# Decay exponents of the mixing loop read from rows of running sums instead of summed by TensorE; another order of the first weight splits

## The reference, cut to what matters

```python
def ssd_scan(xs, dt, da, bm, cm, s0, strict):
    def step(s, inp):
        xc, ac, bc, cc = inp
        acum = jnp.cumsum(ac, axis=1)
        seg = acum[:, :, None] - acum[:, None, :]
        lmat = jnp.exp(jnp.where(mask[None, :, :, None, None], seg, -jnp.inf))
        cb = jnp.einsum('bngs,bmgs->bgnm', cc, bc)
        y_in = jnp.einsum('bgnm,bnmgr,bmgrp->bngrp', cb, lmat, xc)
        ...
```

## Time and profile before

| what | value |
|---|---|
| time, median of 3 runs | 2429.6 us (2429.22 to 2432.43) |
| the profiled execution's own time | 2438.31 us |
| its span, first to last instruction | 2436.7 us |
| busy in the span | PE 2214.0, DVE 1399.9, ACT 1057.1, POOL 649.2 us |
| mean granted TensorE clock | 0.955 of full speed |

### The profile page before, as it was taken

One profiled execution on the slowest core, in us unless ns is written; L12 is line 12 of the kernel. 1 busy time (PEld: TensorE's weight loads), 2 busy tenths in 40 slices (PEclk: granted clock), 3 DMA queues, 4 the chain that ended last, 5 costly groups with the idle time before them and its releaser, 6 DMA issues. The chain is left out here.

```text
span 2436.7 us, 35328 instructions
## 1 busy us (share of the span) xinstructions
PE 2214.0 (91%) x11572; PEld 1840.7 (76%) x11573; DVE 1399.9 (57%) x2063; ACT 1057.1 (43%) x1517; POOL 649.2 (27%) x646
## 2 busy tenths in 40 slices
PE   6999999999998769997999839999999999999990
PEld 3788888899997658886888737777777777777770
DVE  2422222366565658886577644855666664647776
ACT  3432232242223026665222224755665654546763
POOL 0000000000000648886122232322332333223214
PEclk8999999999999889998999959999999999999995
DMA  9433334556552976665553245987988887758997
GB/s 295 174 139 114 112 123 156 188 153 191 177 164 81 346 292 224 224 223 188 177 196 139 104 135 147 339 271 223 323 250 256 268 251 238 220 170 256 347 351 290
DMA packets 302556, 518.78 MB, mean 213 GB/s; under 512 B 38486, under 2 KB 211062, under 8 KB 297704
## 3 DMA queue, kind: packets, MB, share of 16 engines
q1 hardware_dynamic: 276040, 439.52, 53.3%
q0 software_dynamic: 17216, 44.60, 8.4%
q10 hardware_dynamic: 9216, 33.56, 3.4%
HBM read 397.28 MB, written 129.09 MB: 216 GB/s over the span
## 5 line engine op out<-in xcount | busy, mean ns | idle before, releaser
L2381 DVE TENSOR_TENSOR e_w_low<-e_w_whole,e_w_high 128x2048 fp32r<-128x2048 f32 x192 | 431.4, 2289 | 93.3 <-ACT e_w_high L2333 90.0
L2333 ACT ACTIVATE e_w_high<-e_w_whole 128x2048 fp32r<-128x2048 f32 x192 | 356.5, 1907 | 24.3 <-PEq L1676 12.1
L2287 PE MATMUL e_pG<-e_w_high,e_xT 128*128 128x512 f32 x768 | 306.1, 399 | 1.2 <-ACT e_xT L2326 1.2
L2288 PE MATMUL e_pG<-e_w_low,e_xT 128*128 128x512 f32 x768 | 305.9, 398 | 0.0
L808 PE MATMUL proj_acc<-w_high,hT_high 128*128 128x512 f32 x672 | 264.8, 394 | 3.8 <-DVE hT_low L890 3.8
L808 PE MATMUL proj_acc<-w_low,hT_high 128*128 128x512 f32 x672 | 263.1, 391 | 0.0
L808 PE MATMUL proj_acc<-w_high,hT_low 128*128 128x512 f32 x672 | 262.9, 391 | 0.0
L2306 PE MATMUL e_pY<-e_w_high,e_hT 128*128 128x512 f32 x768 | 225.7, 406 | 0.0
L2291 PE MATMUL e_pG<-e_w_high,e_xT 128*128 128x512 f32 x768 | 195.5, 396 | 0.0
L1072 DVE SCALAR_TENSOR_TENSOR conv_out<-ch,cw,conv_out 128x258 f32<-128x258 f32 x288 | 120.5, 485 | 97.7 <-ACT conv_out L719 97.5
L2287 PEld LDWEIGHTS e_pG<-e_w_high,e_xT 128*128 128x128 f32 x768 | 145.7, 190 | 37.2 <-issue 1.6
(11 more groups left out here) (290 smaller groups left out, 4169.9 us busy)
## 6 DMA issues: line engine op xcount, KB each, us to landing
e_w_whole<-in_moe_w_gate_dram SPq DMA_DIRECT2D x64, 1024.0 KB, 8.5
e_w_whole<-in_moe_w_up_dram SPq DMA_DIRECT2D x64, 1024.0 KB, 11.5
e_w_whole<-in_moe_w_down_dram SPq DMA_DIRECT2D x64, 1024.0 KB
by_token<-tok SPq DMA_DIRECT2D x32, 512.0 KB, 3.6
w_in_raw<-in_w_mod_dram SPq DMA_DIRECT2D x32, 512.0 KB, 3.6
m_tok<-by_token SPq DMA_DIRECT2D x16, 768.0 KB, 5.5
s_kv<-by_token SPq DMA_DIRECT2D x20, 512.0 KB, 5.9
modulated_high<-hT_high SPq DMA_DIRECT2D x9, 1024.0 KB, 3.9
```

The costliest lines, as they stand in the source:

```text
L2287: nc.tensor.matmul(pG[:, half], xT[:, 0, k], wh[:, half, w], start=(k == 0), stop=False)
L2288: nc.tensor.matmul(pG[:, half], xT[:, 0, k], wl[:, half, w], start=False, stop=False)
L2333: nc.scalar.activation(wh[:, third, part], raw[:, third, part], ACT.Copy).then_inc(whs.sem, 1)
L2381: nc.vector.tensor_tensor(wl[:, third, part], raw[:, third, part], wh[:, third, part].bitcast(F32), ALU.subtract).then_inc(wls.sem, 1)
```

## The change

1. **Second pass of front.** Behind `dt_sums`, DVE writes the running sums into the table `dd` (forward minus backward, and backward) instead of `da` itself. In turn 1 PE makes two products of 128 columns that give the same sums with heads of a tile along the partitions and tokens along the row (`decay_rows`); DVE copies them out (`rows_of_decays`) and SP writes them to HBM as `decays`.
2. **mixing.** SP loads for each tile the 2 x 1024 sums, each row broadcast to all 128 partitions (`issue_rows`, 1 MB written to SBUF per tile, two slots). ACT makes `relu(row + column)` for the forward excess (`excess`, 8 instructions of 128 x 128), POOL subtracts the column from the backward row (`backward_less`, 128 x 1024) and then the excess (`lesser`, 128 x 1024), and ACT takes the exponential from SBUF. `spread` and the four products of 512 columns are gone.
3. **Clearing.** The 17 clearing DMAs are issued in the second pass of front, not in mixing.
4. **First splits.** Pieces 6 and 7 are split behind the first `modulate` and `low_h`, and DVE copies the fourth modulation row behind piece 4, not behind piece 7.

The diff, cut to its core:

```diff
@@ front, sync
+            def clear(n):
+                if n == 0:
+                    sp.wait_ge(zeroed.sem, zeroed.at(0))
+                if n <= NL:
+                    rows = dram["ys"][n * P:(n + 1) * P, :].rearrange("p (h d) -> p h d", h=2)
+                    sp.dma_start(rows, zero[:].unsqueeze(1).to_broadcast([P, 2, D // 2])).then_inc(ys_out.sem(0), 16)
...
+                if u == 2:
+                    sp.wait_ge(row_sums.sem, row_sums.at(0))
+                    for d in range(2):
+                        sp.dma_start(dram["decays"][d].rearrange("(q n) -> q n", n=P), decay_row[:, d]).then_inc(rows_out.sem(0), 16)
+                clear(2 * u)
                 load_slab(4 * u + 4)
                 store_u(u, 1)
+                clear(2 * u + 1)
@@ front, scalar
-            for n in range(8):
+            for n in range(6):
                 high_first(n)
             act.wait_ge(cols.sem, cols.at(0))
-            for j in range(2):
-                modulate(0, j)
+            modulate(0, 0)
+            for n in (6, 7):
+                high_first(n)
+            modulate(0, 1)
@@ front, tensor
+            def decay_rows():
+                pe.wait_ge(row_sums.sem, 2)
+                for d in range(2):
+                    m = nc.tensor.matmul(two[:, d, 0:P], da[:, d, NCT:].rearrange("p t h -> p (t h)"), g["tri"][:, 2 * d], start=True, stop=True)
+                m.then_inc(sums.sem, 1)
@@ front, vector
             leave_row(2)
-            for n in range(4, 8):
-                low_first(n)
+            low_first(4)
             leave_row(3)
+            low_first(5)
...
-            for j in range(2):
-                low_h(0, j)
+            low_h(0, 0)
+            for n in (6, 7):
+                low_first(n)
+            low_h(0, 1)
...
-                V.tensor_copy(dd[:, :, 2:4], da[:].rearrange("p d t h -> p t d h"))
...
+                V.tensor_copy(g["dd"][:, :, 3], two[:, 1, 0:NS].rearrange("p (t h) -> p t h", t=NT)).then_inc(row_sums.sem, 1)
+                dve.wait_ge(row_sums.sem, 1)
+                V.tensor_tensor(g["dd"][:, :, 2], two[:, 0, 0:NS].rearrange("p (t h) -> p t h", t=NT), g["dd"][:, :, 3], ALU.subtract).then_inc(row_sums.sem, 1)
@@ mixing, sync
+                sp.wait_ge(exps.sem, exps.at(t - 2))
+                issue_rows(s, tile)
...
+            def issue_rows(s, tile):
+                src = dram["decays"][:, (tile - NCT) * SH * P:(tile - NCT + 1) * SH * P]
+                sp.dma_start(rows[:, s].rearrange("p d h n -> p d (h n)"), src.unsqueeze(0).to_broadcast([P, 2, SH * P])).then_inc(rows_in.sem(s), 16)
...
                 load(t, t // 2, t % 2, t + NCT)
-                clear(t)
@@ mixing, gpsimd
-            def spread(t, d):
-                pool.wait_ge(prod.sem, prod.at(t - 1))
-                nc.gpsimd.tensor_tensor(by(dav[:, d], SH), g["tri"][:, 2 * d].unsqueeze(1).to_broadcast([P, SH, P]),
-                                        heads(tile_row(g["dd"], t + NCT, 2 + d), P), ALU.mult).then_inc(davs.sem, 1)
+            def backward_less(t, use, s):
+                pool.wait_ge(rows_in.sem(s), rows_in.at(use))
+                nc.gpsimd.tensor_tensor(rows[:, s, 1], rows[:, s, 1], heads(tile_row(g["dd"], t + NCT, 3), P), ALU.subtract).then_inc(bwd.sem, 1)
+
+            def lesser(t, s):
+                pool.wait_ge(bwd.sem, bwd.at(t))
+                pool.wait_ge(above.sem, above.at(t))
+                nc.gpsimd.tensor_tensor(rows[:, s, 1], rows[:, s, 1], rows[:, s, 0], ALU.subtract).then_inc(less.sem, 1)
@@ mixing, tensor
-                    pe.wait_ge(davs.sem, davs.at(t + 1))
-                    pe.wait_ge(ysum.sem, ysum.at(t, 2))
-                    for half in range(2):
-                        for d in range(2):
-                            m = nc.tensor.matmul(bank[:, 5 + half], g["tri"][:, 1 + 2 * d], dav[:, d, half * 512:(half + 1) * 512], start=(d == 0), stop=(d == 1))
-                    m.then_inc(prod.sem, 1)
@@ mixing, scalar
+            def excess(t, use, s):
+                act.wait_ge(rows_in.sem(s), rows_in.at(use))
+                for h in range(SH):
+                    m = nc.scalar.activation(rows[:, s, 0, h], rows[:, s, 0, h], ACT.Relu,
+                                             bias=g["dd"][:, bass.ds(t + NCT, 1), 2, h:h + 1].rearrange("p a b -> p (a b)"))
+                m.then_inc(above.sem, 1)
...
                 if there(t + 1):
+                    excess(t + 1, use + s, 1 - s)
                     steps(t + 1)
...
-                    act.wait_ge(prod.sem, prod.at(t + 1))
-                    nc.scalar.activation(L[:].rearrange("p h n -> p (h n)"), bank[:, 5:7].rearrange("p a b -> p (a b)"), ACT.Exp).then_inc(exps.sem, 1)
+                    act.wait_ge(yssd.sem, yssd.at(t))
+                    act.wait_ge(less.sem, less.at(t + 1))
+                    nc.scalar.activation(L[:], rows[:, 1 - s, 1], ACT.Exp).then_inc(exps.sem, 1)
```

More of the change, by code:

```diff
@@ L604, in _ @@
             nc.gpsimd.memset(chb[:, :, EXT - 2:EXT], 0.0).then_inc(padded.sem, 1)
+            for j in range(2):
+                pool.wait_ge(qk_out.sem(j), qk_out.at(LAST_TURN))
+                pool.wait_ge(vg_out.sem(j), vg_out.at(LAST_TURN))
+            nc.gpsimd.memset(zero[:], 0.0).then_inc(zeroed.sem, 1)
         @block.scalar
@@ L873, in _ @@
                         dt_sums()
+                    if o == 4 and t == 1:
+                        decay_rows()
                     if o == 3 and t and t % 2 == 0:
@@ L1063, in weights, with rows_of_decays @@
                 m.then_inc(tabs.sem, 1)
+            def rows_of_decays():
+                dve.wait_ge(sums.sem, 2)
+                V.tensor_copy(decay_row[:, 1], two[:, 1, 0:P]).then_inc(row_sums.sem, 1)
+                dve.wait_ge(row_sums.sem, 3)
+                V.tensor_tensor(decay_row[:, 0], decay_row[:, 1], two[:, 0, 0:P], ALU.subtract).then_inc(row_sums.sem, 1)
             def taps(t, b):
@@ L1090, in _ @@
                         weights()
+                    if t == 1 and b == 3:
+                        rows_of_decays()
                     if b == 2 and t and t % 2 == 0:
@@ L1427, in body @@
                 if there(t + 1):
-                    spread(t + 1, 1)
+                    lesser(t + 1, 1 - s)
                     pool.wait_ge(qk_in.sem(1 - s), qk_in.at(use + s))
```

40 lines of the change are left out of this document (21 added, 19 removed).

## The result

| | before | after |
|---|---|---|
| median | 2431.57 us (8 runs, 2428.07 to 2435.79 but for one) | 2440.15 us (8 runs, 2435.55 to 2445.04) |
| ratio of the runs | | 1.0034, 95% interval 1.0022 to 1.0045 |
| profiled execution, own time | 2438.31 us | 2440.07 us |

The ratio is 8.3 us. One run of before, at 2868.42 us, lies 18% above the others and is left out of the ratio. The two profiles differ by 1.8 us only. The one of before lay 8.7 us above the median given ahead of the prediction, the one after lies at its median. Positions in two profiles are no good measure either: from the first product to the first transposes of mixing it takes 831.3 us in the profile of before, and between 823.5 and 832.3 in the twelve profiles that share the new splits.

The account below looks back on a forecast made before the run. A ring of waits through ACT, POOL and DVE (15.24 us a tile), not PE (15.10), was taken to bound mixing. Terms -5.5 + 0.5 + 3 + 6.3 = +4.3 us took the median from 2429.6 to 2434 us, range 2422 to 2445.

Parts of the forecast that it names:

- slower was the likeliest sign: Whole kernel: chances given were slower 0.46, same within 0.2% 0.32, faster 0.22.
- First splits: Start of the kernel: the first product starts at 51 us instead of 56.84, worth -5.5 us.
- the -3 given for loads that come late: First splits: -3 us instead of -5.5 if the loads come late.
- Second pass: Second pass of front: two added PE products of 128 columns cost +0.5 us; DVE's small instructions and clearing DMAs cost nothing.
- Start of mixing: Ahead of tile 0: later rows and `excess` delay PE's transposes 6.6 us, less 3.44 of products gone: +3 us.
- The bound of mixing is a ring, not PE: Steady mixing: a ring of waits takes 15.24 us a tile, PE 15.10; removing 3.44 us of PE is worth next to nothing.
- The ring: Mixing: tiles lengthen from 15.24 to 15.7 us, +0.45 a tile over 14 tiles, +6.3 us.
- The step that failed: Mixing: `excess` uses up ACT's idle 1.3 and 1.5 us ahead of `m_yr`; POOL's extra 0.4 us are mostly covered.
- The 1.1 us that were to come back: Mixing, tile without `w_out`: `m_y` no longer starts beside DVE's `m_t`, giving back 1.1 to 1.2 us.
- Rival 2: Mixing: `lesser` takes 2.5 us and `m_minus_mean` waits for all of it; 16.1 us a tile, +12, 2440 us; chance 0.20.
- Rival 4: Mixing: PE's clock falls in its idle gaps; 2545 us if it stayed low; chance 0.04 that part costs over 5 us.
- POOL's pair at 4.3 us: Mixing: by the skill's floor `backward_less` and `lesser` cost 4.3 us instead of 4.15, the sum 1 us higher.

Follow-up runs that it names:

- run 1: The kernel before with only the new order of the first weight splits; ratio to before 0.9981 (0.9971 to 0.9991).
- run 3: The kernel before without PE's four products of 512 columns per mixing tile, nothing added; first to last ACT square of mixing 228.16 us, before 227.14.
- after_less_short: Also run 4: the changed kernel with `lesser` subtracting a repeated 128 x 128 tile; first to last square of mixing 235.62 us, in the change 235.97.
- run 10: The kernel before with the new first splits and minus mean times `rs` made by POOL instead of DVE; ratio to before 0.9964 (0.9950 to 0.9977).
- run 2: The changed kernel with PE still making the four products per mixing tile, which nobody reads; ratio to before 1.0028 (1.0016 to 1.0039).
- run 6: The changed kernel with one of the eight pieces of ACT's `excess`; first to last square of mixing 238.00 us, in the change 235.97.
- run 5: The changed kernel with `lesser` subtracting a column constant along each row; first to last square of mixing 228.23 us, in the change 235.97.
- run 9: The changed kernel with `m_minus_mean` moved from DVE to POOL, ahead of `lesser`; ratio to before 0.9980 (0.9971 to 0.9990).
- runs 7 and 12: Tile t + 2's `excess` made in ACT's idle time: in the changed kernel (1.0058 to before), and with minus mean on POOL, `m_kd` on ACT (0.9971).

## Why the prediction was right, and where its reasons were not

The time lies inside the range, the ratio puts 2429.6 at 2438, and slower was the likeliest sign. By its steps:

- **First splits, -5.5.** The marker moved by 5.8, the time by 4.6 (-7.1 to -2.2). Right within that interval, which also holds the -3 given for loads that come late.
- **Second pass, +0.5.** The two products are four instructions of 0.27 us, 0.61 us from the first start to the last end (530.20, L885). No run took this part by itself, nor the moved clearing. What is left over of the 12.9 us behind A + B is 0.5, or 1.3 against run 1, less than the uncertainty of the 12.9.
- **Start of mixing, +3.** A grew by 3.6. Its parts: the transposes came 6.0 us later instead of 6.6, and the products gone were worth 3.0 (run 3) where 3.44 was taken; the remaining 0.6 is within what A varies by itself. The rows landed 2.57 behind q and k, for an expected 2.6. The size is in part luck: with the spell at half clock that other runs had here, A would have grown by 5.9, the value of after_less_short.
- **The bound of mixing is a ring, not PE.** Shown by run 3 (PE's 3.44 us removed, tiles not shorter) and from the other side by run 10 (ring shortened, tiles exactly PE's 15.10).
- **The ring, +0.45 a tile.** Without the spells at half clock the change takes (15.31 + 16.06) / 2 = 15.69 (run 2), +0.45 over before. The number is right, and the reasons are right in one of the two tiles. **The step that failed:** "So ACT, which had about 1.3 and 1.5 us of idle time ahead of `m_yr`, becomes part of the ring", with `lesser`'s extra time "mostly covered, since ACT now comes later than POOL". `excess` took 2.45 us instead of 3.09. In the tile without `w_out` ACT therefore does not come later, and `m_yr` waits for `lesser`, 10.08 us behind the square. Cutting `excess` to an eighth left that tile at 16.05 (run 6), and `lesser` at 1.90 put it back to 15.60 (run 5). In the tile with `w_out` ACT did become part of the ring, with `m_yr` at 10.58 instead of the 11.34 forecast, and 4.73 to 4.95 us from there to the square, where 4.75 was forecast. That tile grew by 0.47 without spells (run 2), where the prediction had 1.3.
- The run with the short `lesser` gave back 7.7 of the 8.8 us of B: 4.3 without the spells (232.54 in run 2 against 228.23), of which 1.2 lie in the first tile alone, and 3.4 because the half-clock spells no longer make a square late. The spells are still there in run 5 (clock 0.95). They put `m_minus_mean` 0.2 us later, 8.07 behind the square, and with 1.73 us of its own it is done at 9.80, while ACT's copies hold `m_yr` until 10.58.
- The 1.1 us that were to come back, since `m_y` would no longer start beside `m_t`, did not: in the tile without `w_out` it is 5.97 us from `m_yr` to the next square, where 4.85 was forecast and 6.00 stood in the earlier trace rows. That error and the one on `excess` cancelled, which is luck: forecast 16.1 + 15.25 = 31.35 us for two tiles, with the longer one the tile with `w_out`; measured 15.42 + 16.05 = 31.47, with the longer one the other.
- **Rival 2, `lesser` at 2.5 us, 2440.** This is the mechanism of the tile without `w_out` (2.35 us, all of it waited for by `m_minus_mean`). It was held to be less likely than the forecast. Its tile of 16.1 did not come: 15.69 without spells.
- **Rival 4, PE's clock.** It fell behind seven of the gaps between 895 and 1137 us, and the mean of that stretch is 0.94. It cost 3.4 us in B, above the "covered by the same idle time" of the prediction and below the 5 us of the rival. The gaps were expected at 2 to 2.6 us; they were 1.73 to 1.76 and 2.95 to 3.50. The 2545 us of this rival are also summed wrongly: +8 a tile takes the place of the +6.3, which gives some 2540.
- **POOL's pair at 4.3 us.** The prediction says that by it the sum would be 1 us higher; 4.3 instead of 4.15 us over 14 tiles is some 2 us. It did not enter the sum. Measured, the pair takes 1.89 + 2.35 = 4.24.

So the sum is -4.6 (splits) + 3.6 (start) + 2.8 (`lesser`, waited for in the tiles without `w_out`) + 2.5 (ACT's order or `lesser`, either of which is enough, in the tiles with it) + 0.1 (the last tile) + 3.4 (clock) + 0.5 = +8.3. The last 0.5 is what is left over, so the sum closes by construction. The terms of the ring are run 2 against before, tile by tile.

What stays open: no run of the change took both `lesser`'s length and `excess` away; only the kernel before, which has neither, stands for that. And A was profiled once per kernel, so its terms are good to 1 or 2 us.

## What to carry to other kernels

A full engine next to a ring of waits of about the same length is not the bound until the ring is shorter: before giving work of a full engine to others, follow one tile's waits round, and ask on whose time the replacement lands. Here 3.44 us of PE were exchanged for 0.46 us of POOL, and the 0.46 counted. The cheapest gain was a tiny instruction: 4 columns on DVE that took 1.73 to 2.30 us beside a POOL instruction each tile, where they take 0.16 alone. Moved ahead of that on POOL, it was worth 13 us in the changed kernel and some 4 in the old one. With it the loop of the changed kernel is 2.8 us shorter than that of the old one (B 221.35 and 224.19, runs 9 and 10), so only then was the relief of PE worth something there; but the start takes it back, and the old kernel with the same edit and the splits is the faster of the two (0.9964 against 0.9980, whose intervals overlap). And an instruction moved ahead in a loop is moved ahead in the loop's prologue too, where its data may not have landed (runs 7 and 12).

## What the runs showed of the hardware

- POOL's two-input instruction of 128 x 1024 has two prices here. It takes 1.89 to 1.90 us if an operand is a column that stays the same along each row of a head (`spread`, `backward_less`, run 5), and 2.35 to 2.36 us if both change from element to element, a tile repeated eight times included (`lesser`, run 4). The Trainium skill, "GPSIMD Engine Reference", section "Instruction dispatch", gives 2.5 cycles per element as the floor of a two-input instruction, an estimate of 2.1 us at its clock. The 2.35 us lie above that floor; the 1.90 us lie below it, and there the measurement decides.
- DVE's `m_minus_mean`, with two SBUF operands, waits for the whole of a POOL instruction that began 0.07 us (or, with `w_out`, 0.19 us) earlier: 1.84 and 1.73 us for 4 columns beside `spread`, 2.30 and 2.19 beside `lesser`, against 0.16 alone. It follows the length of POOL's. Negating 4 columns, with one SBUF operand, took 0.17 us, but 0.74 where it began 1.2 us behind the start of POOL's `backward_less` (1033.87 in run 9), and it ended 0.03 behind that: it waited too. The Trainium skill, "SBUF — State Buffer", section "Who interferes with whom", says that an instruction with two SBUF inputs contends with POOL's reads, and that `tensor_scalar` can too, in its 2-port modes; the trace agrees with both, though no row tells the mode.
- TensorE's pairs at 0.63 us instead of 0.38 to 0.39 go with a granted clock of 0.50, the lower of its two levels (1046.90 to 1052.20 in the change). In the change every idle gap of 2.95 to 3.50 us ahead of the products on scores was followed by such pairs within 0.8 us (seven of seven), and none of those of 1.73 to 1.76 us (eight). Over all the traces of mixing here, all 36 gaps of 3.42 to 3.50 us were followed by them, and 16 of 33 between 2.1 and 2.9 us. In the change the spell held 7 or 8 pairs five times and cost 0.1 to 0.2 us of the tile, or nothing; twice it began with the first pair and held all 12, and then the tile took 16.71 and 16.83 us instead of 15.3.
